# A hybrid HGRN2 / differential-attention / RWKV-7 step on one core: the identity products between dependent stages taken out

## What is computed

```python
def hgrn2_mix(...):      # per head: o_t = S_t^T q_t,  S_t = diag(f_t) S_{t-1} + k_t v_t^T
    o = rms_norm(o, norm_g) * sigmoid(hg)
def diff_attn_block(...):
    p = softmax(where(allowed, q @ k^T * DH ** -0.5, NEG_BIG))
    w = p[:, :, 0] - lam * p[:, :, 1]
    return w @ v
def rwkv7_scan(...):     # per token and head
    S = S * w_t + (S a_t) b_t^T + v_t k_t^T ;  y_t = S r_t
```

## Time and profile before

| | us |
|---|---|
| Median of three runs | 6027.74 |
| The three runs | 6043.19, 6027.74, 6021.82 |
| Span of the profiled execution, first to last instruction | 6046.0 |
| Own device time of the profiled execution | not given apart from its span |
| TensorE busy with matmuls, of that span | 5438.2 |
| Mean granted clock of TensorE | 0.899 |
| Busy with filler matmuls | 431.0 |

### The profile page before, as it was taken

How to read it: one execution, slowest core, us unless ns; L and a number is a source line. 1 busy time by engine, 2 the same in 40 slices (tenths; PEclk the granted TensorE clock), 3 DMA queues, 4 the chain that set the end, 5 groups by cost and what they waited for, 6 DMA issues and landing times.

```text
span 6046.0 us, 82156 instructions
## 1 busy us (share of the span) xinstructions
PE 5438.2 (90%) x33415; PEld 4602.2 (76%) x33415; DVE 2075.5 (34%) x3008; ACT 992.5 (16%) x1207; POOL 262.7 (4%) x449
## 2 busy tenths in 40 slices
PE   7787878787999998899899999999999987999988
PEld 5566565676999996588778777777787777999977
DVE  2424242413333332400435435345354324333331
ACT  2212121102111112000111201201112003112121
POOL 1101111010000000200000000000000000000000
PEclk9989898988999999999979779788797798999999
DMA  2202121120111111121000000000000011111111
GB/s 60 70 26 63 34 54 42 30 67 21 43 46 43 43 38 32 31 75 68 25 17 15 3 15 3 17 15 3 17 15 3 1 37 32 43 46 43 43 35 51
DMA packets 305827, 206.22 MB, mean 34 GB/s; under 512 B 26664, under 2 KB 290782, under 8 KB 305438
## 3 DMA queue, kind: packets, MB, share of 16 engines
q1 hardware_dynamic: 290302, 161.38, 9.3%
q0 software_dynamic: 11584, 25.97, 1.6%
q10 hardware_dynamic: 3552, 13.41, 0.6%
HBM read 173.66 MB, written 27.04 MB: 33 GB/s over the span
## 4 chain that ended last, share of the span: by engine, by line
issue 40%; PE 34%; PEld 9%; DVE 6%; ACT 3%; POOLq 2%; DVEq 2%; PEldq 1%; ACTq 1%; POOL 1%; DMA 0%; SPq 0%
PE ps L1226 33%; PEld ps L1226 9%; DVE big L772 3%; ACT big L520 2%; POOLq L257 1%; DVE big L862 1%; DVEq L1151 1%; PE ps L1295 1%; POOLq L470 1%; ACT L520 0%; POOL big L259 0%; ACTq L612 0%; POOLq L259 0%; DVE big L919 0%; ACT xa L520 0%
## 5 line engine op out<-in xcount | busy, mean ns | idle before, releaser
L1226 PE MATMUL ps<-parts,wparts 128*128 128x272 f32 x12288 | 1558.8, 289 | 83.1 <-DVEq L993 83.1
L1226 PEld LDWEIGHTS ps<-parts,wparts 128*128 128x128 f32 x12288 | 1557.0, 190 | 84.7 <-DVEq L993 84.7
L1226 PE MATMUL ps<-big 128*128 128x128 f32 (+5 forms) x7960 | 1303.1, 319 | 179.8 <-ACTq L612 44.4
L1226 PEld LDWEIGHTS ps<-big 128*128 128x128 f32 (+2 forms) x7960 | 1070.7, 206 | 346.4 <-issue 80.9
L520 ACT ACTIVATE big<-ps 64x128 f32<-64x128 f32 (+6 forms) x434 | 252.4, 594 | 2964.8 <-PE ps L1226 1860.3
L1226 PE MATMUL ps<-xa,ring 128*128 128x272 f32 (+2 forms) x2496 | 681.2, 434 | 57.5 <-issue 43.6
L1226 PEld LDWEIGHTS ps<-xa,ring 128*128 128x128 f32 x2496 | 454.8, 192 | 283.8 <-issue 214.1
L1226 PE MATMUL ps<-big,ring 128*128 128x272 f32 (+4 forms) x2848 | 631.3, 383 | 35.0 <-DVEq L1053 20.1
L1226 PEld LDWEIGHTS ps<-big,ring 128*128 128x128 f32 (+3 forms) x2848 | 505.1, 181 | 160.5 <-issue 29.3
L772 DVE TENSOR_TENSOR big<-ps,big 128x512 f32<-128x512 f32 (+5 forms) x436 | 259.0, 603 | 555.6 <-PE ps L1226 299.3
L1226 PE MATMUL ps<-ident,ones 128*128 128x128 f32 x3072 | 431.0, 297 | 3.0 <-DVEq L861 3.0
(11 more groups left out here) (179 smaller groups left out, 3114.8 us busy)
## 6 DMA issues: line engine op xcount, KB each, us to landing
ring<-in_mlp_up SPq DMA_DIRECT2D x64, 512.0 KB, 4.0
ring<-in_mlp_down SPq DMA_DIRECT2D x64, 512.0 KB, 3.8
ring<-in_w_in_even SPq DMA_DIRECT2D x28, 512.0 KB, 7.0
rkv_scratch<-big ACTq DMA_DIRECT2D x24, 544.0 KB, 4.4
big<-rkv_scratch SPq DMA_DIRECT2D x24, 544.0 KB, 4.5
big<-in_cache_k SPq DMA_DIRECT2D x128, 64.0 KB, 1.9
big<-in_cache_k POOLq DMA_DIRECT2D x128, 64.0 KB, 2.2
big<-in_cache_v SPq DMA_DIRECT2D x128, 64.0 KB, 1.9
```

Of the source, the lines that this page charges most:

```text
L1226: return pe.matmul(out, lhsT, rhs, start=start, stop=stop, skip_group_check=True)
```

## The change

Every call of `warm` and the function itself are taken out of the tensor program. Waits, real products, their order and the programs of the other four engines are the same. The diff, cut to one or two lines for each place (the line numbers are those of before):

```diff
-            def warm(b, n):
-                for _ in range(n):
-                    mm(bank(b, P), ones[:, :], ident[:, :])
...
-                warm(0, 3)
                 pe.wait_ge(gram_used, i * 9 + 8)
                 rows_of(1, e["T1"]).then_inc(kdt_done, 1)
                 pe.wait_ge(gram_used, i * 9 + 9)
-                warm(0, 7)
                 pe.wait_ge(kdt_ok, i + 1)
...
-                warm(0, 10)
                 pe.wait_ge(states_ok, i + 1)
...
-                warm(5, 6)
                 pe.wait_ge(o_sq, i + 1)
...
-                warm(6, 16)
                 pe.wait_ge(rinv_ok, i + 1)
                 rows_of(1, e["DK"]).then_inc(ko_done, 1)
-                warm(6, 7)
                 pe.wait_ge(ko_ok, i + 1)
...
-                    warm(2, 8 if qb == 0 else 3)
                     pe.wait_ge(w_ok, i * 8 + qb + 1)
...
-                    warm(2, 2)
                     pe.wait_ge(wt_ok, i * 12 + done + (1 if qb < 4 else 2))
...
-                warm(6, 10)
                 pe.wait_ge(rw_act, i * 6 + 1)
...
-                warm(6, 16)
                 pe.wait_ge(rw_act, i * 6 + 4)
                 wide(1, headones[:, :], w["RN"]).then_inc(rw_mm, 1)
-                warm(6, 12)
                 pe.wait_ge(rw_dve, i * 6 + 4)
                 wide(0, headones[:, :], w["LW"]).then_inc(rw_mm, 1)
-                warm(6, 22)
                 pe.wait_ge(rw_dve, i * 6 + 5)
...
-                warm(6, 8)
                 pe.wait_ge(rw_trc, i * 4 + 4)
...
-                    warm(6, 6)
                     pe.wait_ge(gr_used, i * 18 + h * 9 + 9)
...
                         p1(1, lv)
-                        if lv == 0:
-                            warm(3, 8)
                         if lv < RWL - 1:
                             p1(0, lv + 1)
-                        else:
-                            warm(3, 4)
...
                     last.then_inc(akv_done, 1)
-                    warm(3, 5)
...
-                warm(3, 5)
                 pe.wait_ge(y_ok, i + 1)
                 wide(0, headones[:, :], w["YS"]).then_inc(gn_mm, 1)
...
-                warm(6, 10)
                 pe.wait_ge(gn_act, i * 2 + 1)
                 wide(0, headones[:, :], w["SQ"]).then_inc(gn_mm, 1)
-                warm(6, 16)
                 pe.wait_ge(so_ok, i + 1)
                 pe.wait_ge(gn_act, i * 2 + 2)
```

## The result

The changed kernel took 6152.4 us (median of four runs, 6126.3 to 6170.4) against 6035.5 us for the kernel before on the same chip: a ratio of 1.0188, 95% interval 1.0153 to 1.0224, or about +117 us. The forecast was 6089 us, with 5990 to 6175 as its range. The direction was right, and the loss was about twice the size forecast. The profiled execution of the changed kernel has a span of 6146.1 us, 100.1 us above that of before.

A forecast was written before the change was run, and what follows sets the result against it. Hand-over between engines was taken to bound the kernel, TensorE's work being under half the path. The core's +66 us (eight trips of +8.3) and the even trips' -5 gave +61: 6089 us beside the median, range 5990 to 6175.

The forecast's parts named there:

- Gram blocks: RWKV core, both heads: a fifth of the full price of running at 1.2 GHz, +1.5 and +1.6 us a trip.
- rival 2: RWKV core: gram blocks at 1.2 GHz in most trips, +5 to +7.75 us per head, total 6120 to 6188 us; chance 0.18.
- Start of the inverse: RWKV core, behind the gram blocks: unfilled pause lets the clock fall for a stretch, +2.2 us per head, between 0 and 5.
- Preparation and tail: RWKV trip's stages outside gram blocks, inverse and scan: lower clock against overhang gained, 0.6 + 1.0 a trip, 13 us in all.
- gate product: RWKV preparation: 4.91 us becomes 8.5 at 1.2 GHz, +3.6; with 2.6 gained by starting earlier, +1.0 a trip.
- mean of squares: RWKV tail: 2.15 us now, at either clock level after a pause; between 0 and +2.1, taken as +0.8 a trip.
- head mean: RWKV tail: 3.15 us becomes 3.6 at the lower clock; with 1.1 gained by starting earlier, -0.6 a trip.
- overhang: Filler still running when the awaited work is done; ahead of the gate product its removal was to gain 2.6 us.
- sum over the keys: RWKV preparation: 1.5 us gained and at most 2.1 lost, hanging on the gate's copy, so counted as 0.
- Even mixer: Even trips, chunk states to attention: overhang gained against lower clock, -1.3 us a trip, by four trips -5 us.
- Rival 1: RWKV core: the clock holds through the short pauses, gram blocks and inverse cost nothing, 5986 to 6018 us; chance 0.17.
- the first 18 instructions of the inverse: Sign at the inverse's start: 3.8 us where they take 2.31; still 2.3, with clock 1.00 up to the scan, means Rival 1.

The follow-up runs named there:

- trimmed kernel: Kernel before with two preparation calls cut, ahead of the gate product from 10 to 6 and behind it from 16 to 9: 1.0014, +7 us.
- all five calls: Kernel before without the five filler calls around the gram blocks and the inverse of the RWKV core, preparation and tail keeping theirs: 1.0110, +68 us.

## Why the prediction was wrong in size

By its own steps, in the order of its sum:

- **Gram blocks, the step that failed.** The recorded prediction took "a fifth of the full price for each: +1.5 and +1.6", 25 us in all. The traces show 27.8 + 20.1 = 48 us, as eleven of sixteen blocks ran at the low clock. The bounds of the price (+5 to +7.75) held for a block that stays there all the time (5.3 and 6.2 us at 0.52 and 0.51) and were too high for the rest (3.5 to 4.0 us at 0.58 to 0.60). What was wrong was the share. The reasoning was that the transposes just ahead lift the clock. They do, and a block even begins at 1.00. But behind the pause of 1.46 us it falls within the block, and the 64-row products don't lift it again: in none of the 72 slow blocks in the traces of all kernels does it return before the last of them. This is rival 2, which had a chance of 0.18. That the measured time lies between its bounds is in part luck: the gram blocks alone would have made 6112 us, under its 6120. Of the 56 us between +61 and +117 they are 23; preparation and tail are 18 and the even mixer 17 by their runs, and the start of the inverse takes 3 back.
- **Start of the inverse: right.** Forecast +2.2 per head, 35 us; by the trace 32 us; alone on the chip +31 us.
- **Preparation and tail: right in sign, too small.** The gate product took 9.31 us where 8.5 was taken, the mean of squares 3.84 where 2.95 was taken (2.15 + 0.8), the head mean 4.10 where 3.6 was. Forecast 13 us for both stages (0.6 + 1.0 a trip); by the traces +23 without the last trip's tail, and on the chip +31. At the gate product the overhang was subtracted in full although part of it bought the product its clock, as the trimmed kernel shows. The sum over the keys was rightly counted as 0.
- **Even mixer: open.** Forecast -5 us; +12 us (6 to 20) on the chip, so the sign was wrong. In the traces of before and after the core begins within 0.3 us of the same time, so the execution in the trace shows neither a gain nor a loss in the even trips. The cause of the +12 us is open.
- **Rival 1, the clock holds, is out.** The Trainium skill's "TensorE: Matmul & The Clock Gate", section "Why this matters for your kernels", warns of long idle gaps; here short pauses sufficed. With the call ahead of head 0 out, a pause of 1.5 to 1.65 us stands there and five of eight blocks fell; with the two ahead of head 1 out, 0.81 us stands just ahead of it (the other call was inside the inverse before it), and seven of eight fell. Its section "Part 4: PE-mode transpose" says that transposes don't count for the clock. The traces still disagree: in the fourth trip of the changed kernel TensorE idles for 4.98 us, runs only transposes from 3706.20 on, and the clock came back among them (0.50 up to 3708.50, 0.87 from there to 3712.50). The consequence that the prediction drew from that section, a low clock in the gram blocks of head 0, came all the same, by another way.
- What was to show it: the clock was 0.845 (forecast: under 0.899), the preparation 0.59 ("about 0.6"), the first 18 instructions of the inverse 4.18 us (forecast 3.8), the gram blocks "13 or more", which the prediction named as the sign of rival 2.

What stays open: why head 1 keeps its clock in six trips of eight without all five calls, but in one without the two ahead of it. Within one kernel the blocks that fell and those that held had the same instructions ahead of them; they differ in where they lie in time, and in the clock that those instructions ran at. No run separates this.

## What to carry to other kernels

Where the clock is in play, price a stage by the clock it would get, and ask of each stage whether its own products bring the clock back: half-height products here didn't in 15 us, the dense full-height ones of the inverse did. Whether something else than their height is the reason, such as their 256 columns, no run separates. A filler should carry full-width work, has to stand in the last pause ahead of the stage that it protects, and is worth removing only if it costs more than that stage gains. Fillers left behind a stage that has lost its clock run at 1.2 GHz themselves and make it longer. And look for the stage that runs at the low clock with no filler at all, even where TensorE never waits: fillers in the scan gave 95 us, where all 1536 fillers of before together give 117.

## What the runs showed of the hardware that wasn't expected

- A TensorE that is busy without a gap can stay at 1.2 GHz: 17.21 us with 36 half-height products and 12 fillers, 16 us with twelve gate instructions and 32 narrow fillers, and 61.30 us in the scan of before, where six full-size filler instructions per chunk hold it at 1.00.
- A 128x8 product takes as long as a 128x128 one in such a row of fillers, 0.12 and 0.115 us at full clock; at 1.2 GHz the narrow one takes 0.22 us.
- The same trip runs in two lengths, 239.1 and 242.5 us, within one execution.
